# Seven block products instead of eight for the gate and up projections of a two-block transformer kernel

## The reference, cut to what matters

```
def swiglu(h, w1, w3, w2):
    return (jax.nn.silu(h @ w1) * (h @ w3)) @ w2      # h 256x1024, w1 and w3 1024x2816, w2 2816x1024
```

## Time and profile before

| | before |
|---|---|
| median of 3 runs | 2272.77 us (2272.24 to 2274.1) |
| the profiled execution | 2274.54 us, of which the span is 2272.5 us |
| TensorE busy | 2211.6 us, 97% of the span |
| DVE busy | 766.8 us, 34% |
| ACT busy | 356.2 us, 16% |
| GpSimd busy | 118.8 us, 5% |
| mean granted TensorE clock | 0.987 |

### The profile page before, as it was taken

One profiled execution on the slowest core, in us unless ns is written; L12 is line 12 of the kernel. 1 busy time (PEld: TensorE's weight loads), 2 busy tenths in 40 slices (PEclk: granted clock), 3 DMA queues, 4 the chain that ended last, 5 costly groups with the idle time before them and its releaser, 6 DMA issues.

```text
span 2272.5 us, 23963 instructions
## 1 busy us (share of the span) xinstructions
PE 2211.6 (97%) x10232; PEld 1871.7 (82%) x10232; DVE 766.8 (34%) x1601; ACT 356.2 (16%) x667; POOL 118.8 (5%) x231
## 2 busy tenths in 40 slices
PE   7999999999999999999999999999999999999997
PEld 4777888868888888888788888888888868888886
DVE  6454333313334122336433422332233543340002
ACT  3233200022000100023140200020002223120001
POOL 0100011100111000100000000000010000000000
PEclk9999999999999999999999999999999999999998
DMA  9673576825767565643434465656564433444331
GB/s 357 226 259 102 213 267 245 311 79 186 270 248 295 220 230 199 254 147 146 162 111 148 157 231 200 236 195 231 213 231 154 154 148 111 148 148 148 137 127 70
DMA packets 61539, 438.27 MB, mean 193 GB/s; under 512 B 6976, under 2 KB 8768, under 8 KB 39552
## 3 DMA queue, kind: packets, MB, share of 16 engines
q1 hardware_dynamic: 28608, 318.35, 38.4%
q0 software_dynamic: 32256, 117.45, 13.9%
q10 hardware_dynamic: 576, 1.05, 0.1%
HBM read 434.72 MB, written 2.10 MB: 192 GB/s over the span
## 4 chain that ended last, share of the span: by engine, by line
PE 97%; DVE 1%; ACT 1%; issue 0%; DMA 0%; SPq 0%; ACTq 0%; DVEq 0%
PE lin L1460 79%; PE small_ps L1460 4%; PE lin L1775 2%; PE lin L1718 1%; PE small_ps L1794 1%; PE lin L1528 1%; PE lin L1732 1%; PE small_ps L1564 1%; PE small_ps L1685 1%; PE lin L1672 1%; PE lin L1740 1%; PE small_ps L1766 0%; PE pstat L1472 0%; PE lin L1600 0%; PE small_ps L1615 0%; PE lin L1587 0%
## 5 line engine op out<-in xcount | busy, mean ns | idle before, releaser
L1460 PE MATMUL lin<-h,ring 128*128 128x256 f32 x5424 | 1180.3, 380 | 5.4 <-ACT h L807 2.8
L1460 PEld LDWEIGHTS lin<-h,ring 128*128 128x128 f32 x5424 | 1030.0, 190 | 150.7 <-issue 9.2
L1460 PE MATMUL lin<-big,ring 128*128 128x256 f32 x2112 | 457.4, 379 | 7.9 <-DVE big L1422 7.9
L1460 PEld LDWEIGHTS lin<-big,ring 128*128 128x128 f32 x2112 | 400.8, 190 | 64.5 <-DVE big L1422 10.3
L871 DVE CUSTOM_DVE_ANT_0 ada_ring<-ada_ring,crow 128x1024 f32<-128x1024 f32 x224 | 268.2, 1219 | 26.7 <-DMA ada_ring<-in_ada 26.1
L1422 DVE TENSOR_TENSOR big<-sil,lin 128x256 f32<-128x256 f32 x112 | 47.1, 421 | 592.8 <-ACT sil L835 592.8
L464 POOL DMA_DIRECT2D ada_ring<-in_ada x224 | 118.3, 528 | 1592.9 <-DVE sums L871 1561.0
L1012 DVE SCALAR_TENSOR_TENSOR x<-lin,mod,x 128x256 f32<-128x256 f32 x80 | 38.7, 483 | 449.3 <-PE lin L1460 424.2
L835 ACT ACTIVATE sil<-lin 128x256 f32<-128x256 f32 x112 | 42.9, 383 | 723.2 <-PE lin L1460 723.2
L1460 PE MATMUL lin<-rec,ring 128*128 128x257 f32 (+1 forms) x608 | 148.2, 397 | 7.8 <-ACT rec L532 7.8
L1460 PEld LDWEIGHTS lin<-rec,ring 128*128 128x128 f32 x608 | 120.8, 199 | 28.5 <-issue 9.6
(11 more groups left out here) (296 smaller groups left out, 1175.1 us busy)
## 6 DMA issues: line engine op xcount, KB each, us to landing
ring<-in_w SPq DMA_DIRECT2D x66, 2048.0 KB, 8.3
ada_ring<-in_ada POOLq DMA_DIRECT2D x224, 512.0 KB, 5.6
ring<-in_w SPq DMA_DIRECT2D x48, 1408.0 KB, 6.1
ring<-in_gates SPq DMA_DIRECT2D x12, 2048.0 KB, 7.9
ring<-in_mproj SPq DMA_DIRECT2D x8, 2048.0 KB, 8.0
ring<-in_mtok SPq DMA_DIRECT2D x4, 2048.0 KB, 7.7
ring<-in_branch SPq DMA_DIRECT2D x4, 2048.0 KB, 7.8
ring<-in_wout SPq DMA_DIRECT2D x4, 2048.0 KB, 7.8
```

What stands on the lines that cost most here:

```text
L1460: ins = mm(dst, w[:, lo:lo + m], rhs(k), start=k == 0, stop=k == nk - 1)
```

## The change

It replaces units 4 to 21 of w13 in all six layers, 18 tiles, by 9 chunks. A chunk is one block of weights: gate and up of two tiles. Tokens are cut in two halves of 128, the 1024 features in two halves of 512, the columns in two tiles (each with its gate and up, 256 columns). This is a 2x2 by 2x2 product of blocks, done with seven block products instead of eight (Winograd's form). A product is 4 matmuls with h (or a sum of its quarters) stationary and 256 weight columns moving; the result is token-major, so the hidden tiles are turned on TensorE (4 transposes for a chunk) and copied to `big` by ACT.

- Sums of h's quarters: four DVE additions of 128x512 in a layer (`combine_h`), behind unit 2.
- Sums of weight quarters, 128x1024 each: for each chunk two on GpSimd (`combine`) and then two on DVE (`combine_twice`), one chunk ahead, in two sets of buffers.
- DVE adds the products up (`chunk`): 9 operations of 128x256 for a chunk, in order with waits between, two of them writing PSUM. ACT does a copy of the first product, a copy of the turned tiles (128x512) and two silus for a chunk.
- TensorE's order in a chunk: products 1, 2, the turning of the chunk before, 3, 5, 6, 7, 4 (`gate_and_up`). The last chunk's turning goes into the first unit of w2, behind 16 of its 22 products.
- ada blocks are spread anew: 42, 38, 29, 32, 33 and 0 in the six layers and 18 in the fourier sublayer, ahead of its `residual`. Their issue on the GpSimd queue goes between the sums.
- A weight slot is free for its next load when product 5 of its chunk ends.

```diff
 ADA_BEFORE_CONTEXT, ADA_BEFORE_KEYS, ADA_AFTER_KEYS = 2, 15, 9
 ADA_IN_MLA = ADA_N - FIRST_GATE + ADA_N
-ADA_PER_FFN = [48, 48, 32, 32, 32, 0]
+ADA_IN_UNITS = [3, 2, 2, 2, 2, 0]
+ADA_IN_CHUNKS = [[3] * 3 + [2] * 6, [2] * 9, [1] * 9, [2] * 9, [2] * 4 + [1] * 5, [0] * 9]
+ADA_IN_RESULTS = [[3] * 6, [3] * 6, [3] * 6, [2] * 6, [3] * 6, [0] * 6]
+ADA_IN_FOURIER = 18
+ADA_PER_FFN = [a + sum(b) + sum(c) for a, b, c in zip(ADA_IN_UNITS, ADA_IN_CHUNKS, ADA_IN_RESULTS)]
+CHUNKS = KF // 2 - RAW // 2
...
+        first_kept, partial_2, partial_3, first_gate, first_up, second_gate = [att[:, i] for i in range(6)]
+        def product_bank(s, n):
...
+            place = {1: pa[2], 2: pa[1], 3: pa[3], 5: pa[0], 6: lin[after % NBANK], 7: lin[(after + 1) % NBANK],
+                     4: lin[(after + 2) % NBANK]}
+            return place[n][:, 0:T]
...
             pool.wait_ge(s_ada_first_dma[FIRST_N - 1], 16)
-            for n in range(ADA_N * len(subs) - FIRST_GATE):
-                if n >= ADA_SLOTS:
-                    pool.wait_ge(s_ada_used, n - ADA_SLOTS + 1)
-                pool.dma_start(ada_ring[n % ADA_SLOTS][:], I["ada"][n]).then_inc(s_ada_dma[n % ADA_SLOTS], 16)
...
+            def combine(ph, f, j):
+                n, done = ph.first + RAW // 2 + j, f * CHUNKS + j
+                if j:
+                    pool.wait_ge(s_fourth_product, done - 1)
+                    pool.wait_ge(s_sixth_product, done)
+                else:
+                    pool.wait_ge(s_unit, ph.unit0 + 2)
+                pool.wait_ge(s_weights[n % SLOTS], (n // SLOTS + 1) * 16)
+                b11, b12, b21, b22 = [quarter(n % SLOTS, c, half) for half in range(2) for c in range(2)]
+                W = nc.gpsimd.tensor_tensor
+                W(combined_weights(j, 0), b12, b11, ALU.subtract).then_inc(s_weights_combined, 1)
+                W(combined_weights(j, 2), b22, b12, ALU.subtract).then_inc(s_weights_combined, 1)
+                ada_issue(ada_before(f) + ADA_IN_UNITS[f] + sum(ADA_IN_CHUNKS[f][:j]))
+            for s, kind in enumerate(subs):
+                if kind == "ffn":
+                    f = ffn_before(s)
+                    ada_issue(ada_before(f))
+                    for j in range(CHUNKS):
+                        combine(by_name[s, "w13"], f, j)
+            ada_issue(ADA_N * len(subs))
...
                     u0 = unit0[s, "w13"]
-                    for n in range(KF):
+                    f = ffn_before(s)
+                    for n in range(RAW):
                         if folded(s) and n < RAW:
...
                         else:
                             act.wait_ge(s_unit, (u0 + n) + 1)
                             A(sil[:, n % 2], lin[(u0 + n) % NBANK][:, 0:T], ACT.Silu).then_inc(s_silu, 1)
+                    for j in range(CHUNKS + 1):
+                        if j < CHUNKS:
+                            act.wait_ge(s_first_product, nth(act, s_first_product))
+                            if j:
+                                act.wait_ge(s_first_up, nth(act, s_first_up))
+                            A(first_kept, product_bank(s, 1), ACT.Copy).then_inc(s_first_kept, 1)
+                        if j:
+                            act.wait_ge(s_second_gate, nth(act, s_second_gate))
+                            A(second_gate, second_gate, ACT.Silu).then_inc(s_second_gate_silu, 1)
+                            act.wait_ge(s_hidden_turned, nth(act, s_hidden_turned))
+                            at = RAW + 2 * (j - 1)
+                            A(big[:, at:at + 2], pstat[:].rearrange("p (a b) -> p a b", a=2), ACT.Copy).then_inc(s_hidden_kept, 1)
+                        if j < CHUNKS:
+                            act.wait_ge(s_first_gate, nth(act, s_first_gate))
+                            A(first_gate, first_gate, ACT.Silu).then_inc(s_first_gate_silu, 1)
+                    nth(act, s_first_up)
...
+            def combine_h(s):
+                dve.wait_ge(s_h_ready, KD * (s + 1))
+                a11, a12, a21, a22 = [quarter_of_h(half, tt) for tt in range(2) for half in range(2)]
+                s1, s2, s3, s4 = [combined_h(i) for i in range(4)]
+                V.tensor_tensor(s1, a21, a22, ALU.add).then_inc(s_h_combined, 1)
+                V.tensor_tensor(s3, a11, a21, ALU.subtract).then_inc(s_h_combined, 1)
+                dve.wait_ge(s_h_combined, nth(dve, s_h_combined))
+                V.tensor_tensor(s2, s1, a11, ALU.subtract).then_inc(s_h_combined, 1)
+                dve.wait_ge(s_h_combined, nth(dve, s_h_combined, 2))
+                V.tensor_tensor(s4, a12, s2, ALU.subtract).then_inc(s_h_combined, 1)
+                nth(dve, s_h_combined)
+            def combine_twice(s, j):
+                n, made = by_name[s, "w13"].first + RAW // 2 + j, ffn_before(s) * CHUNKS + j
+                b21, b22 = quarter(n % SLOTS, 0, 1), quarter(n % SLOTS, 1, 1)
+                dve.wait_ge(s_weights_combined, 2 * made + 1)
+                V.tensor_tensor(combined_weights(j, 1), b22, combined_weights(j, 0), ALU.subtract).then_inc(s_weights_combined_twice, 1)
+                dve.wait_ge(s_weights_combined_twice, nth(dve, s_weights_combined_twice))
+                V.tensor_tensor(combined_weights(j, 3), b21, combined_weights(j, 1), ALU.subtract).then_inc(s_weights_combined_twice, 1)
+                nth(dve, s_weights_combined_twice)
+            def chunk(s, j):
+                def added(dst, a, b, signal=s_dve_chain, early=0):
+                    if early:
+                        dve.wait_ge(s_hidden_turned, nth(dve, s_hidden_turned))
+                    V.tensor_tensor(dst, a, b, ALU.add).then_inc(signal, 1)
+                    dve.wait_ge(signal, nth(dve, signal))
+                dve.wait_ge(s_second_product, nth(dve, s_second_product))
+                dve.wait_ge(s_first_kept, nth(dve, s_first_kept))
+                V.tensor_tensor(first_gate, product_bank(s, 2), first_kept, ALU.add).then_inc(s_first_gate, 1)
+                dve.wait_ge(s_sixth_product, nth(dve, s_sixth_product))
+                added(partial_2, product_bank(s, 6), first_kept)
+                added(first_up, product_bank(s, 5), partial_2, early=j)
+                added(product_bank(s, 3), product_bank(s, 3), first_up, s_first_up)
+                dve.wait_ge(s_first_gate_silu, nth(dve, s_first_gate_silu))
+                V.tensor_tensor(first_up, product_bank(s, 3), first_gate, ALU.mult).then_inc(s_taken_by_dve, 1)
+                dve.wait_ge(s_seventh_product, nth(dve, s_seventh_product))
+                added(partial_3, product_bank(s, 7), partial_2)
+                dve.wait_ge(s_fourth_product, nth(dve, s_fourth_product))
+                V.tensor_tensor(second_gate, product_bank(s, 4), partial_3, ALU.add).then_inc(s_second_gate, 1)
+                added(product_bank(s, 5), product_bank(s, 5), partial_3)
+                dve.wait_ge(s_second_gate_silu, nth(dve, s_second_gate_silu))
+                V.tensor_tensor(second_gate, product_bank(s, 5), second_gate, ALU.mult).then_inc(s_taken_by_dve, 1)
+                if j == CHUNKS - 1:
+                    nth(dve, s_hidden_turned)
...
                     if name == "w2":
-                        ada(share(ADA_PER_FFN[ffn_before(s)] * 3 // 8, KD - 2, m))
+                        ada(ADA_IN_RESULTS[ffn_before(s)][m] if m < KD - 2 else 0)
...
                 if kind == "fourier":
+                    ada(ADA_IN_FOURIER)
                     residual(s, "wf")
                 if kind == "ffn":
-                    ffn = subs[:s].count("ffn")
+                    ffn = ffn_before(s)
                     u0 = unit0[s, "w13"]
-                    for n in range(KF):
+                    for n in range(RAW):
...
-                        ada(share(ADA_PER_FFN[ffn] * 5 // 8, KF - 2, n - 2) if n > 1 else 0)
+                        if n == 2:
+                            combine_h(s)
+                            combine_twice(s, 0)
+                    ada(ADA_IN_UNITS[ffn])
+                    for j in range(CHUNKS):
+                        chunk(s, j)
+                        if j + 1 < CHUNKS:
+                            combine_twice(s, j + 1)
+                        ada(ADA_IN_CHUNKS[ffn][j])
                     residual(s, "w2")
...
+            def gate_and_up(s):
+                ph, f = by_name[s, "w13"], ffn_before(s)
+                u0, before = ph.unit0, ffn_before(s) * CHUNKS
...
+                def turn_hidden(j):
+                    pe.wait_ge(*taken(u0 + RAW + 2 * j + 1))
+                    if j:
+                        pe.wait_ge(s_hidden_kept, before + j)
+                    for a in range(2):
+                        for tt, tokens in enumerate((first_up, second_gate)):
+                            at = a * T + tt * P
+                            ins = turn(pstat[:, at:at + P], tokens[:, a * P:(a + 1) * P])
+                    ins.then_inc(s_hidden_turned, 1)
+                h_tile(KD - 1)
+                pe.wait_ge(s_h_combined, 4 * (f + 1))
```

(120 more changed lines are left out.)

## The result

| | before | changed |
|---|---|---|
| median, first measurement | 2273.26 us (4 runs) | 2203.59 us (2197.33 to 2206.36, 4 runs) |
| ratio, 95% interval | | 0.969 (0.9669 to 0.9711) |
| median, second measurement | 2273.9 us (9 runs) | 2199.12 us (2198.33 to 2200.83, 5 runs) |
| ratio, 95% interval | | 0.9672 (0.9659 to 0.9685) |
| profiled execution, its span | 2274.54, 2272.5 | 2197.33, 2195.5 |

What follows compares the result with a forecast made beforehand. TensorE, 97% busy, was taken to bound the kernel. Six layers save 54.7 us, less 2.4 for late turnings and 0.5 for fourier: 51.8 us, from 2274.54 profiled to 2222.7, median 2221 us; range 2214 to 2247.

Steps and rivals of the forecast that it cites:

- TensorE's sum, turning: TensorE's work in a chunk: 12.09 us of matmuls plus 0.875 us for 4 transposes, 12.96 us in all.
- Products and the hole before w2: 56 records a chunk cost 12.09 us, weights moving priced like h moving; TensorE's gap between w13 and w2 goes.
- The turning's lateness: Transposes wait for ACT's silu and DVE's product: 0 to 0.1 us late, 0.05 us taken for 48 turns, 2.4 us.
- Product 5: It waits for all four weight sums; wanted at 6.05 us, possible at 5.7 to 5.95, so no lateness taken.
- Rival B: A chain is late in every chunk: 0.35 us in 54 chunks, 19 us more, 2238 us; chance 22%.
- DVE behind it and GpSimd: In a chunk DVE is busy 8.9 of 12.96 us and doesn't bound; GpSimd sums of 2.2 us stay hidden.
- rival C: DVE's additions of the products stand while GpSimd sums, turning 1.5 us late: slower, 2291 us; chance 8%.
- Fourier: Fourier sublayer: 18 ada blocks through three slots may end late, up to 1.8 us; 0.5 us taken.

Runs made afterwards that it cites:

- turning by products: Changed kernel with each chunk's four transposes done as ordinary products with the identity: 2219.61 us, ratio 0.976 to the kernel before.
- split wait: Changed kernel with product 5 waiting only for GpSimd's weight sums, product 6 for DVE's, slot released at product 6: 2194.48 us, 0.966 of the kernel before.
- early sum: Changed kernel with DVE's first weight sum of the next chunk put ahead of DVE's last product: 2194.73 us, 0.9649 of the kernel before.
- early GpSimd pair: Changed kernel with GpSimd's two weight sums no longer waiting for product 6 of the chunk before: 2211.97 us, 0.973 of the kernel before.

## Why the prediction was wrong

**TensorE's sum, turning: the step that failed.** The term of the turning was taken at twice its size. I wrote "4 transposes, 8 records", carrying over that a 32-bit product is two records. The rows that I priced it by were right, 0.109 us a record. But the 16 records there are 16 transposes. A count would have shown it: what the trace had of a known number of transposes (64 records at L1564 where the first sublayer turns 64 blocks) was there to be read. A chunk's turning measured 0.44 us, not 0.875, and over 54 chunks the forecast was 54 x 0.4375 = 23.6 us too dear. The turning by products, where there are 8 records, gave the forecast's cycle (12.98 us) and 2219.6 us.

**Products and the hole before w2**: right. 56 records of 0.2158 us a chunk with weights moving; nothing between w13 and w2.

**The turning's lateness**: I took 2.4 us; it is nothing. The silu from SBUF took 0.41 us where I put 0.51, so DVE's product ended at 3.14 of the cycle where I had 3.21, and the turning started at 3.46. The margin, 0.32 us from DVE's end to the turning, is inside the 0.06 to 0.34 that I had for a handover, so it was near.

**Product 5**: the place was right, the room wrong through the same miscount. I had it wanted at 6.05 us of the cycle and possible at 5.7 to 5.95. It was wanted at 3.45 + 0.44 + 1.73 = 5.62 and came, its slower records counted, at about 5.75, 0.14 us late, 6.7 us in 48 chunks. Rival B named this chain, at 0.35 us.

**DVE behind it and GpSimd**: right. A GpSimd sum is 2.36 us, between 0.9 and 2.6 and near the 2.2 taken. The estimate of 2.2 us from the Trainium skill's page "GPSIMD Engine Reference" (section "Elementwise — side-by-side cycle accounting") is as near. DVE's additions from PSUM stayed at 0.42 us while GpSimd summed, so rival C didn't happen. Its mechanism exists, but here only operations with SBUF inputs alone showed it, and in the chunks the order of the change keeps them apart.

**Fourier**: taken 0.5 us with 1.8 as bound; TensorE waited 1.84 us there in the first profile and 1.3 in the second, about 1.0 us more than taken.

**The sum again**: 51.8 + 23.6 + 2.4 - 6.7 - 1.0 = 70.1 us. Measured are 69.7 and 74.8. The stage itself closes: 54.7 + 23.6 - 6.7 = 71.6 us, and in the traces 754.8 - 680.5 less 2.6 us for the turnings in w2 is 71.7. Most of the rest is the clock behind the norms, which was not in my sum. At each norm TensorE has 3.34 us with only two records to do; its next 16 records then took 5.40 us (granted clock 0.68 over those shown first) or 3.72 (1.00). The chain of before, and that of the changed kernel, both around the fifth feed-forward layer's end:

```profile
1505.10 0.14 issue
1505.23 5.40 PE lin L1460 x16
```

```profile
1455.70 0.14 issue
1455.84 3.72 PE lin L1618 x16
```

The profile of before has all five such starts at 5.40 us; the profiles of the changed kernel two of five each, 1.6 to 1.7 us apiece. The first product of the fourier sublayer's transform shows the same (32 records in 15.7 us before and 14.0 in the first profile after, though not in the second). That is 5 to 7 us of the profile's gain of 77.2. It also accounts for most of the spread among the experiments' profiles: above 3.72 us in sum, the five starts had 3.2 us in the changed kernel's second profile, 6.3 in the turning by products, 4.8 in the split wait and 9.5 in the early sum. Taken off, the profiled executions differ from the changed kernel by 17.1, -6.1 and -7.2 us, where 16.9, -6.7 and -6.7 were expected. These five are not all: records near 41 and 92 us and the fourier product vary by up to 1.7 us as well. Free of them is the sum over the stretches from the first chunk to w2: 680.6 us in the changed kernel, 673.9 with the split wait and 673.7 with the early sum. What decides how a start goes when the wait in front of it is the same, was not tried and stays open.

## What to carry to other kernels

Before pricing an operation by its records, count the records of a known number of such operations, for each operation by itself: on this chip's 32-bit data a product had two and a transpose one. When a stage is shortened, take its new times through every other chain that ends in it; the 0.44 us saved at the turning made the next wait late. An engine with a third of its time free can still be too late at one place, and the remedy is to wait there for less or to do the work earlier.

## What the runs showed of the hardware

- A DVE sum of two SBUF tiles stood while a GpSimd sum ran: 2.94 us for a 1.22 us sum. In the changed kernel a DVE operation with one SBUF tile and per-partition scalars (x from xc, 128x256) took 2435 ns in three of 40 cases, beside a GpSimd sum, and 403 ns otherwise; additions from PSUM with one SBUF tile kept 0.42 us.
- Waits of 2.2 us in every chunk cost TensorE granted clock as well, 0.93 over the stretch and 1.7 us in each of 35 of 48 chunks; waits of 1.63 us in the last layer (early GpSimd pair) left the 24 records behind them at 5.18 us.
- After stretches of the same length, 3.34 us with two records in them, TensorE's clock had fallen at two places of one execution of the changed kernel (5.40 and 5.34 us for 16 records) and not at three others (3.72); in the kernel before it had fallen at all five.
